# Encoder step on one core: the tiles of two attention groups in alternating lengths, the differential group's maps scored one after the other

## The reference

```python
def _layer(h, p_l, past, ...):
    xn = _rmsnorm(h, g_attn)
    aq, ak, av, bq, bk, bv, cq, ck, cv, dq, dk, dv, dlogf = _project(xn, w_in, b_f)
    ...
    a_out = _stick_breaking(aq, a_k, a_v, q_pos, k_pos)
    b_out = _swa_prompt(...)            # window of 128 keys, with sinks and a position bias
    c_out = _diff_attention(cq, c_k, c_v, q_pos, k_pos, lam, rel_bias)
    c_out = _rmsnorm(c_out, diff_gain) * (1.0 - lam_init)
    d_out = _forgetting_attention(dq, d_k, d_v, q_pos, k_pos, f_cum[:, -s:], f_cum)
    h = h + concat(a_out, b_out, c_out, d_out) @ w_out
    h = h + jnp.square(jax.nn.relu(_rmsnorm(h, g_mlp) @ w_up)) @ w_down
    h = h + jax.nn.sigmoid(h @ w_ple_gate) * (p_l @ w_ple_proj)
...
# stick-breaking (A): w = exp(log_sigmoid(z) + sum over newer keys of -softplus(z))
# differential (C):   w = softmax(s0) - lam * softmax(s1), two maps of 32 columns each
# forgetting (D):     softmax(s + f_query - f_key)
```

## Time and profile before

| what | value |
|---|---|
| median of 3 runs | 1962.59 us (1962.41 to 1962.87) |
| the profiled execution | 1961.66 us |
| its span | 1959.9 us |
| mean granted clock of TensorE | 0.969 |
| TensorE matmul busy over the span | 93% |
| VectorE, ScalarE, GpSimd busy | 43%, 33%, 4% |
| the attention stage | 359.2 to 870.9 us of the span |

### The profile page before, as it was taken

One profiled execution on the slowest core, in us unless ns is written; L12 is line 12 of the kernel. 1 busy time (PEld: TensorE's weight loads), 2 busy tenths in 40 slices (PEclk: granted clock), 3 DMA queues, 4 the chain that ended last, 5 costly groups with the idle time before them and its releaser, 6 DMA issues. The chain is left out here.

```text
span 1959.9 us, 27322 instructions
## 1 busy us (share of the span) xinstructions
PE 1828.4 (93%) x10459; PEld 1637.6 (84%) x10459; DVE 850.5 (43%) x1619; ACT 650.0 (33%) x1387; POOL 85.1 (4%) x169
## 2 busy tenths in 40 slices
PE   6999998588889999979989999999999999998998
PEld 6999996477777787868889898989898989996886
DVE  4333331666665666543543333333333333333434
ACT  5322321566554444442332121212121222221335
POOL 0000000000000010011010000000000000000000
PEclk9999999699899999979989999999999999999999
DMA  5666841756456745625231111111111111112102
GB/s 178 210 226 218 269 170 67 154 122 138 97 121 146 146 103 132 148 60 184 70 126 44 43 44 44 43 44 43 43 43 44 43 43 43 43 44 66 50 28 99
DMA packets 152165, 195.20 MB, mean 100 GB/s; under 512 B 42980, under 2 KB 106148, under 8 KB 152024
## 3 DMA queue, kind: packets, MB, share of 16 engines
q1 hardware_dynamic: 105352, 131.63, 25.8%
q10 hardware_dynamic: 39136, 36.05, 5.5%
q0 software_dynamic: 7552, 25.76, 4.0%
HBM read 143.17 MB, written 54.81 MB: 101 GB/s over the span
## 5 line engine op out<-in xcount | busy, mean ns | idle before, releaser
L113 PE MATMUL up<-xt_hi,w_hi_even 128*128 128x384 f32 x768 | 258.0, 336 | 2.0 <-PEq L1444 1.8
L115 PE MATMUL up<-xt_hi,w_lo_even 128*128 128x384 f32 x768 | 257.8, 336 | 0.0
L114 PE MATMUL up<-xt_lo,w_hi_even 128*128 128x384 f32 x768 | 257.6, 335 | 0.0
L115 PE MATMUL down<-w_hi_odd_b,hidden_lo 128*128 128x512 f32 x576 | 224.5, 390 | 0.0
L114 PE MATMUL down<-w_lo_odd_b,hidden_hi 128*128 128x512 f32 x576 | 224.5, 390 | 0.0
L113 PE MATMUL down<-w_hi_odd_b,hidden_hi 128*128 128x512 f32 x576 | 224.0, 389 | 0.0
L1665 DVE TENSOR_TENSOR h_rows<-down,h_rows 128x1024 f32<-128x1024 f32 x72 | 88.2, 1225 | 236.8 <-PE down L115 236.8
L1630 ACT ACTIVATE hidden_rows<-up 128x384 f32<-128x384 f32 x96 | 47.3, 492 | 418.0 <-PE up L115 418.0
L1658 DVE TENSOR_TENSOR hidden_rows<-hidden_rows 128x384 f32<-128x384 f32 x96 | 53.6, 558 | 224.3 <-ACT hidden_rows L1630 224.3
L113 PEld LDWEIGHTS up<-xt_hi,w_hi_even 128*128 128x128 f32 x768 | 145.0, 189 | 3.6 <-DVE xt_lo L140 2.2
L114 PEld LDWEIGHTS up<-xt_lo,w_hi_even 128*128 128x128 f32 x768 | 145.0, 189 | 0.8
(11 more groups left out here) (264 smaller groups left out, 3522.0 us busy)
## 6 DMA issues: line engine op xcount, KB each, us to landing
w_raw<-w_up SPq DMA_DIRECT2D x64, 256.0 KB, 2.9
w_raw<-w_down SPq DMA_DIRECT2D x64, 256.0 KB, 3.2
w_raw<-w_in SPq DMA_DIRECT2D x24, 256.0 KB, 4.5
head_rows<-head_out ACTq DMA_DIRECT2D x16, 288.0 KB, 3.8
head_rows_in<-head_rows POOLq DMA_DIRECT2D x9, 512.0 KB, 4.4
x_rows<-x_prompt SPq DMA_DIRECT2D x8, 512.0 KB, 3.6
w_raw<-w_out SPq DMA_DIRECT2D x16, 256.0 KB, 5.5
residual_rows<-x_prompt POOLq DMA_DIRECT2D x16, 256.0 KB, 3.2
```

What stands on the lines that cost most here:

```text
L113: nc.tensor.matmul(out, xh, wh, start=first, stop=False)
L114: nc.tensor.matmul(out, xh, wl, start=False, stop=False)
L115: return nc.tensor.matmul(out, xl, wh, start=False, stop=last)
```

## The change

- **Order.** The first job keeps its order 0 to 8. A's and D's other jobs take the tiles 0, 4, 1, 5, 8, 6, 2, 7, 3; B's and C's take 0, 1, 2, 3, 4, 8, 5, 6, 7, with 8 the sample's. The functions go by `tile(i)` in place of `i % TILES`. What belongs to a job's end (norm, store) goes by the last tile and no longer by the sample. The last `turn_back` behind TensorE's loop goes.
- **C's maps.** In tiles of more than 512 keys, TensorE first waits for map 0's bank, does its 4 products and its bias, and then does the same for map 1. Before, it waited for both and issued the products in pairs.
- **keep_moving.** For C it is 3 matmuls in every tile, no longer 7 in tiles 4 to 7.
- **Semaphores.** They are no longer raised; waits for zero are left out. `primed_sem` goes.
- **First job's loads.** Queries and keys come in columns 0 to 511 (6 loads) and then the rest (6 loads); tile 0 waits for the first six, tile 4 for the others.
- **VectorE.** In A, the sample's output is read between the first and the second pass of `stick_breaking`.
- **GpSimd.** The squares of a C head come ahead of the next job's `spread_new`, and the rest of its norm behind it.

```diff
+            FIRST_ORDER = list(range(TILES))
+            LONG_LAST = [0, 1, 2, 3, 4, SAMPLE, 5, 6, 7]
+            IN_TURNS = [0, 4, 1, 5, SAMPLE, 6, 2, 7, 3]
+
+            def order(job):
+                if not 0 < job < len(JOBS):
+                    return FIRST_ORDER
+                return IN_TURNS if JOBS[job][0] in "AD" else LONG_LAST
+
+            def tile(i):
+                return order(i // TILES)[i % TILES]
...
             def is_sample(i):
-                return i % TILES == SAMPLE
+                return tile(i) == SAMPLE
...
-            def at(name, k):
-
-                return (TILES if name == "o_full" else 1) + k
+            def after(eng, name, k):
+
+                if k > 0:
+                    eng.wait_ge(q[name], k)
```

SyncE:

```diff
-                    sp.wait_ge(primed_sem, 1)
...
+                                if job == 0:
+
+                                    for cols, loaded in ((slice(0, 512), first_in), (slice(512, TILES * P), done)):
+                                        for part, to in ((0, at_hi), (1, at_lo)):
+                                            sp.dma_start(kt[to:to + half, x, cols].bitcast(F32), k2[g][part][of_k, cols]).then_inc(loaded, 16)
+                                            sp.dma_start(qt[0][to:to + half, x, cols].bitcast(F32), q2[g][part][of_q, cols]).then_inc(loaded, 16)
+                                        for part, to in ((1, at_hi), (0, at_lo)):
+                                            sp.dma_start(qt[1][to:to + half, x, cols].bitcast(F32), q2[g][part][of_q, cols]).then_inc(loaded, 16)
+                                    continue
```

GpSimd:

```diff
-                    for name in NAMES:
-                        pool.sem_inc(q[name], TILES if name == "o_full" else 1)
-                    pool.sem_inc(primed_sem, 1)
...
                         for job in range(len(JOBS)):
+                            of_c = job and JOBS[job - 1][0] == "C"
+                            if of_c:
+                                squares(job - 1)
                             spread_new(job)
+                            if of_c:
+                                norm(job - 1)
                             if job + 1 < len(JOBS):
                                 spread_operands(job + 1)
-                            if JOBS[job][0] == "C":
-                                norm(job)
```

VectorE, in `stick_breaking`:

```diff
                         nc.vector.scalar_tensor_tensor(b, z, 0.0, b, ALU.max, ALU.add).then_inc(q["a_sp"], 1)
-                        dve.wait_ge(q["a_sp"], at("a_sp", k + 1))
-                        dve.wait_ge(q["a_ready"], at("a_ready", max(k - 1, 0)))
+                        if between is not None:
+                            out(between)
+                        after(dve, "a_sp", k + 1)
+                        after(dve, "a_ready", max(k - 1, 0))
```

TensorE, in `scores`:

```diff
+                        if i == 0:
+                            pe.wait_ge(first_in, 16 * 6)
+                        if (i == 4 if job == 0 else t == 0):
+                            job_loaded(pe, job)
...
-                        befores = [score_before(UNIT[(i, m)]) for m in maps]
-                        for x in befores:
+                        def bank_free(m):
+                            x = score_before(UNIT[(i, m)])
                             if x < 0:
-                                pe.wait_ge(q["e_ready"], at("e_ready", 0))
-                            elif group(UNITS[x][0]) == "A":
-                                pe.wait_ge(q["a_logw"], at("a_logw", tiles_before(UNITS[x][0], "A") + 1))
-                            elif x == max(befores):
-                                pe.wait_ge(q["e_ready"], unit_at("e_ready", *UNITS[x]))
+                                return
+                            if group(UNITS[x][0]) == "A":
+                                after(pe, "a_logw", tiles_before(UNITS[x][0], "A") + 1)
+                            else:
+                                after(pe, "e_ready", unit_at("e_ready", *UNITS[x]))
...
+                        if g == "C" and n > 512:
+
+
+                            for m in maps:
+                                bank_free(m)
+                                products([m])
+                                add(m)
+                            return
+                        for m in maps:
+                            bank_free(m)
```

TensorE, in `keep_moving` and behind the loop:

```diff
-                        g, t = group(i), i % TILES
-                        wide = 4 <= t < SAMPLE
+                        g, t = group(i), tile(i)
...
-                        for _ in range({"A": 3 if t >= 3 else 1, "B": 2, "C": 7 if wide else 3, "D": 0}[g]):
+                        for _ in range({"A": 3 if t >= 3 else 1, "B": 2, "C": 3, "D": 0}[g]):
...
-                        turn_back(NT - 1)
```

More of the change, by code:

```diff
@@ L794, in first_block @@
             def first_block(i):
-                return i % TILES - keys(i) // P + 1
+                return tile(i) - keys(i) // P + 1
             UNITS = [(i, m) for i in range(NT) for m in range(2 if group(i) == "C" else 1)]
@@ L893, in job_loaded @@
                 e = job % 2
-                eng.wait_ge(q[f"job_in{e}"], at(f"job_in{e}", 16 * sum(loads(JOBS[x][0]) for x in range(e, job + 1, 2))))
+                after(eng, f"job_in{e}", 16 * sum(loads(JOBS[x][0]) for x in range(e, job + 1, 2)))
             def small_loaded(eng, job):
                 e = job % 2
-                eng.wait_ge(q[f"small_in{e}"], at(f"small_in{e}", 16 * sum(small_loads(JOBS[x][0]) for x in range(e, job + 1, 2))))
+                after(eng, f"small_in{e}", 16 * sum(small_loads(JOBS[x][0]) for x in range(e, job + 1, 2)))
             def banks(i, scalar):
@@ L928, in body @@
                             half, n = HALF[g], P * cached(g)
-                            sp.wait_ge(q["o_full"], at("o_full", TILES * (job - 1)))
+                            after(sp, "o_full", TILES * (job - 1))
                             if g in "BC":
@@ L1312, in scores @@
-                            pe.wait_ge(q[f"ks_in{e}"], at(f"ks_in{e}", 16 * sum(cache_loads(JOBS[x][0]) for x in range(e, job + 1, 2))))
+                            after(pe, "spread", 3 * (job + 1))
+                            after(pe, f"ks_in{e}", 16 * sum(cache_loads(JOBS[x][0]) for x in range(e, job + 1, 2)))
                         maps = range(2 if g == "C" else 1)
                         n_own = {m: (slice(HD * m, HD * m + HD) if g == "C" else slice(0, P)) for m in maps}
-                        befores = [score_before(UNIT[(i, m)]) for m in maps]
@@ new lines, in add, with products @@
+                        def add(m):
+                            for c, unit_, mat in added(i):
+                                last = nc.tensor.matmul(score(i, m)[:, c:c + mat.shape[-1]], unit_, mat, start=False, stop=True, skip_group_check=True)
+                            last.then_inc(q["s_full"], 1)
+                        def products(turns):
+                            k0 = P * first_block(i)
+                            for c in range(0, n, 512):
+                                w = min(512, n - c)
+                                for part in range(2):
+                                    for m in turns:
+                                        own = n_own[m]
+                                        nc.tensor.matmul(score(i, m)[:, c:c + w], qt[part][own, e, P * t:P * (t + 1)],
+                                                         kt[own, e, k0 + c:k0 + c + w], start=part == 0, stop=False, skip_group_check=True)
@@ L1331, in scores @@
                         else:
-                            k0 = P * first_block(i)
-                            for c in range(0, n, 512):
-                                w = min(512, n - c)
-                                for part in range(2):
-                                    for m in maps:
-                                        own = n_own[m]
-                                        nc.tensor.matmul(score(i, m)[:, c:c + w], qt[part][own, e, P * t:P * (t + 1)],
-                                                         kt[own, e, k0 + c:k0 + c + w], start=part == 0, stop=False, skip_group_check=True)
+                            products(maps)
                         for m in maps:
-                            for c, unit_, mat in added(i):
-                                last = nc.tensor.matmul(score(i, m)[:, c:c + mat.shape[-1]], unit_, mat, start=False, stop=True, skip_group_check=True)
-                            last.then_inc(q["s_full"], 1)
+                            add(m)
                     def turn_back(i):
-                        pe.wait_ge(q["ot_read"], at("ot_read", i // TILES + 1))
-                        pe.wait_ge(q["o_read"], at("o_read", i))
+                        after(pe, "ot_read", i // TILES + 1)
+                        after(pe, "o_read", i)
                         nc.tensor.transpose(OP[:, HD * (i % 2):HD * (i % 2 + 1)], ot[:, :], ident[0:HD, 0:HD]).then_inc(q["o_full"], 1)
```

134 lines of the change are left out of this document (70 added, 64 removed).

## The result

The changed kernel takes 2000.2 us (median of 4 executions, 1998.5 to 2003.2), the kernel before 1962.5 beside it: a ratio of 1.0200, 95% interval 1.0179 to 1.0222. I had forecast 1959, with 1949 to 1968 as the range. The profiled execution: 2000.84 us, span 1998.7 (+38.8), mean granted clock 0.954 for 0.969.

A forecast was written before the change was run, and what follows sets the result against it. VectorE was taken to bound A jobs, TensorE B, C and D. Gains at the start, C and D pairs and the end, less A and B and clock losses, summed to -3.7: 1962.6 to 1959 us by median, range 1949 to 1968.

The forecast's parts named there:

- start, to the end of the first job: Opening loads and first job: earlier first scores, limited by the wait for cached rows; -6.2 us, bounds -4.3 and -8.9.
- B of the first pair: First B job: takes its own sample's values without relief from A's new order; +1.3 us.
- three A and B pairs, with their clock: Later A and B pairs: order costs +4.1, +1.9 and +0.6 us, lower clock +4.5 more.
- C and D pairs one to three: C and D jobs before the last pair: shorter by 0.5, 1.3 and 1.1 us.
- last pair and end: Last C and D jobs: the end becomes a tile of four blocks; 80.7 to 73.7 us, -7.0.
- behind the attention: Everything after the attention stage: expected to stay unchanged, 0 us.
- three low pieces: One lower-clock stretch in each of three changed A and B pairs, 1.5 us each, +4.5 (0 to 10).
- Rival 1: Slower: clock falls in every changed A job behind a 4.3 us stop; +8.1 us more, 1967; chance 0.22.
- C's edits: C's long tiles: fewer keep_moving, single maps, height changes and shorter waits together give -1.5 us a job (-6 to +2).
- the gain of 3.7 from fewer keep_moving: C's long tiles: four matmuls fewer save 0.93 us in each of 4 tiles, -3.7 a job.
- The waits I summed to 2.3: TensorE's waits in a D job in turns, including 0.6 us for the next C job's bias; 1.8 before.
- the stop at B's last values: A's opening: TensorE stands some 4.3 us until VectorE reads the output behind the five-block tile at position 1.

The follow-up runs named there:

- the filled kernel: Changed kernel with eight keep_moving matmuls added in D ahead of C's first scores, where TensorE stood 2.0 to 2.1 us: 1984.0 us, ratio 1.0130 to the kernel before.
- Moving the bias: Changed kernel with the next C job's bias done in D one tile earlier, behind position 6 instead of 7: 1997.5 us, ratio 1.0205 to the kernel before.
- the stop filled: Changed kernel with fourteen 512-column matmuls in each A job where TensorE stands for the output behind position 1: 1994.9 us, ratio 1.0174 to the kernel before.
- the start alone: Kernel before with only raised semaphores removed and the first head's queries and keys loaded in two halves: 1956.3 us, ratio 0.9987.
- split waits: Kernel before with new start and three keep_moving in C, first job's value rows loaded early and waited for apart from cached rows: 1948.0 us, ratio 0.9935.
- C's edits alone: Kernel before with the new start, C's long-tile maps one by one and three keep_moving instead of seven, all tiles ascending: 1982.8 us, ratio 1.0139.

## Why the prediction was wrong

The forecast, term by term, against stretches of the profiled executions:

| term | predicted | measured |
|---|---|---|
| start, to the end of the first job | -6.2 | -8.9 |
| B of the first pair | +1.3 | +0.3 |
| three A and B pairs, with their clock | +6.6 + 4.5 | +6.3 + 3.4 + 4.2 = +13.9 |
| C and D pairs one to three | -0.5 - 1.3 - 1.1 | +12.9 + 10.6 + 10.6 = +34.1 |
| last pair and end | -7.0 | +1.4 |
| behind the attention | 0 | -2.0 |
| sum | -3.7 | +38.8 |

(The second pair of C and D: 48.81 + 30.50 = 79.3 for 42.02 + 26.67 = 68.7.)

**The step that failed: the clock.** I gave three low pieces to A and B, 2.0 us to the last pair and nothing to the later C and D pairs, though D in turns got more stops by my own count. With the filled kernel as the measure of full clock (C 39.9, D 30.5) the low clock costs 5.2 and 4.7 in the first pair, 8.9, 8.5 and 7.7 in the other C jobs: an estimate of 35.0 of the 45 us by which C and D missed the forecast. That the clock costs it is shown by removing it: eight matmuls gave 8.9, 8.5 and 7.3 back in these three jobs, of which one D job took 7.1. The orders of C and D suffice for it; the kernels with C and D ascending and pairs held 1.0 in 16 of their 21 later C jobs (seven profiles). Rival 1 had the mechanism and the wrong place: it put 8.1 us more on A and B, where the clock cost 1.7 an A job, and none on C.

**C's edits: -1.5 a job predicted, 0 measured.** Three keep_moving: 41.5 for 42.4, -0.9. One map at a time: +2.3. The single maps were priced about rightly (full pitch at 0.24 and 0.12; a long tile's scores 2.7 to 3.2 for 1.6 to 2.0, where I had 2.2 to 2.9). What failed is the gain of 3.7 from fewer keep_moving: with pairs it gave 0.9, because the waits for the exponentials, which the matmuls had covered, came up in its place (0.96 to 1.23 us ahead of every long tile and the sample's, before 0 to 0.98). Together at clock 1.0: 42.4 for 42.4. The Trainium skill, "TensorE: Matmul & The Clock Gate", "Why this matters for your kernels", says that a short stack of rows alone costs what all rows cost; the 0.24 agrees.

**D: 28.8 predicted, 30.5 at full clock.** The waits I summed to 2.3; they are 0.47, 0.47, 1.07, 0.47 and 2.0. The last was put at 0.6, because I counted the bias and not the four blocks' gates (0.75) and maxima (0.69) behind it. Moving the bias gave 1.2 of it back. With C at 39.9 for 38.6, a pair at full clock is 70.4, not 67.4: with the order's own waits the exchange of places loses 1.9 to before's 68.5 even if the clock holds.

**A and B were nearly right.** A took 37.6 at clock 1.0 (with the stop filled), as forecast to 0.1, and B 20.5 for 20.8. The 0.1 is partly luck: the stop at B's last values, forecast at 4.3, was 3.27. With the low clock A took 39.3, and C's wait for its loads went from 4.85 to 4.7 only (3.7 forecast). The order in turns lost time there even at full clock, as forecast: the way of a long tile is now covered by a short one only.

**Start: right about the cause of its limit.** I said that the values would stand 3.5 us for the cached rows; they stood 3.35. With the start alone the second job began 6.4 earlier; in the other profiles with this start it began 3.7 to 9.1 earlier, so the forecast 6.2 lies well and the -8.9 is partly a draw. Yet the start alone measures only -2.5 us of the whole (-6 to +1): in its profile the last D job begins 0.4 earlier, and the third C job has 10.2 us at half clock. With split waits the stop is gone and the first job takes 31.5 for 34.6.

**Open.** What makes the clock fall in one opening and not in the next: D's stop of 2.0 is not needed (0.87 and 0.48 did, and with C's edits alone 0.47), the same wait of 0.92 in C's middle goes with a fall in one kernel and without in another, and the filling moved the fall in one kernel from C to D. That it is the kind of matmuls ahead and not the waits was never tested by itself. Runs of the same kernel differ in it. Why single maps with three keep_moving lose the clock for so much longer than either edit alone was not tried further. An opening filled in C and D both was not tried.

## What to carry to other kernels

Cost a reordering twice: at full clock by its waits, and again for stretches at half clock that it may bring, for they can cost several times the wait (here 8.9 us behind one of 2.1). Compare the granted clock job by job before explaining any longer stretch; a few useless matmuls in a stop are the cheapest test, but check the next opening, where the fall may reappear. When a filling helps, look in the trace whether it lies in the wait that it was meant for. An earlier start is worth only as much as the next wait lets through: follow the loads to the second consumer and give it a wait of its own.

## What the runs showed of the hardware

The granted clock fell with no wait of TensorE over 0.47 us in the 16.9 us ahead (second C job with C's edits alone, then 34.2 us at 0.5) and behind waits of 0.87 and 0.48 (C behind D with the bias moved, 13.6 us at 0.5), and it held through waits of 1.0 to 1.2 us in every long tile of C (three keep_moving, clock 1.0 over 41.5 us). The Trainium skill, same page and section, names idle gaps between bursts as what drops the clock; the first of these falls had none, so here gaps are not the only cause, and the length of a stop does not tell where the clock falls. Identical work took 55.6 us at a clock of 0.69 and 42.4 at 1.0 in one execution, and one kernel's executions spread over 35 us by it.
